# The last layer norm of a two-block transformer kernel: GpSimd takes part of the subtractions, scalings and affine steps, and the stores go out in another order

## What is computed

```python
def layernorm(x, g, b):
    xf = x.astype(jnp.float32)
    mu = jnp.mean(xf, axis=-1, keepdims=True)
    var = jnp.mean(jnp.square(xf - mu), axis=-1, keepdims=True)
    y = (xf - mu) * lax.rsqrt(var + LN_EPS)
    return (y * g + b).astype(x.dtype)
...
    hid = jnp.square(jax.nn.relu(jnp.einsum('bsd,df->bsf', x, w_ff1)))
    ff = jnp.einsum('bsf,fd->bsd', hid, w_ff2)
    return layernorm(DEEPNORM_ALPHA * x + ff, ln2_g, ln2_b)
```

## Time and profile before

| | us |
|---|---|
| median of 3 runs (2074.2 to 2076.59) | 2075.11 |
| the profiled execution | 2075.19 |
| its span | 2073.4 |
| TensorE busy | 2037.0 |
| VectorE busy | 1233.0 |
| ScalarE busy | 977.0 |
| GpSimd busy | 299.3 |

### The profile page before, as it was taken

One profiled execution on the slowest core, in us unless ns is written; L12 is line 12 of the kernel. 1 busy time (PEld: TensorE's weight loads), 2 busy tenths in 40 slices (PEclk: granted clock), 3 DMA queues, 4 the chain that ended last, 5 costly groups with the idle time before them and its releaser, 6 DMA issues. The chain is left out here.

```text
span 2073.4 us, 26672 instructions
## 1 busy us (share of the span) xinstructions
PE 2037.0 (98%) x10608; PEld 1719.8 (83%) x10608; DVE 1233.0 (59%) x1978; ACT 977.0 (47%) x1606; POOL 299.3 (14%) x279
## 2 busy tenths in 40 slices
PE   9999999999999999999999999999999999999997
PEld 6888788888888888788788799898788788899896
DVE  6655566555443444476576475577676586466576
ACT  5664344334232332366357263464566357264363
POOL 0000000000000000254000234130354000233220
PEclk9999999999999999999999999999999999999999
DMA  7332223333332322633332241332532331242331
GB/s 242 98 106 63 82 62 101 122 102 121 103 102 95 98 92 62 179 107 96 100 102 80 82 140 62 104 122 63 167 110 84 117 102 62 82 142 62 122 102 41
DMA packets 201528, 211.51 MB, mean 102 GB/s; under 512 B 7803, under 2 KB 181115, under 8 KB 201404
## 3 DMA queue, kind: packets, MB, share of 16 engines
q1 hardware_dynamic: 194544, 194.13, 29.9%
q0 software_dynamic: 6352, 15.24, 2.8%
q10 hardware_dynamic: 508, 0.43, 0.1%
HBM read 194.55 MB, written 8.95 MB: 98 GB/s over the span
## 5 line engine op out<-in xcount | busy, mean ns | idle before, releaser
L678 PE MATMUL ps<-Phi,wh 128*128 128x512 f32 (+1 forms) x992 | 393.3, 396 | 5.0 <-DVE x_fvv L1343 2.0
L681 PE MATMUL ps<-Phi,wl 128*128 128x512 f32 (+1 forms) x992 | 372.6, 376 | 0.6 <-DVE wl L1257 0.6
L679 PE MATMUL ps<-Plo,wh 128*128 128x512 f32 (+1 forms) x992 | 371.8, 375 | 0.0
L1257 DVE TENSOR_TENSOR wl<-stage,wh 128x1024 fp32r<-128x1024 f32 (+1 forms) x246 | 305.6, 1249 | 65.4 <-ACT wh L2089 46.7
L2089 ACT ACTIVATE wh<-stage 128x1024 fp32r<-128x1024 f32 (+3 forms) x249 | 251.0, 1020 | 98.0 <-PE ps L681 76.1
L678 PE MATMUL ps<-Qhi,wh 128*128 128x512 f32 (+1 forms) x664 | 254.5, 383 | 9.0 <-DVE Qlo L1276 9.0
L679 PE MATMUL ps<-Qlo,wh 128*128 128x512 f32 (+1 forms) x664 | 253.0, 381 | 0.0
L681 PE MATMUL ps<-Qhi,wl 128*128 128x512 f32 (+1 forms) x664 | 252.7, 381 | 0.0
L678 PEld LDWEIGHTS ps<-Phi,wh 128*128 128x128 f32 x992 | 187.3, 189 | 46.6 <-issue 12.4
L681 PEld LDWEIGHTS ps<-Phi,wl 128*128 128x128 f32 x992 | 186.7, 188 | 35.8 <-DVE wl L1257 1.0
L679 PEld LDWEIGHTS ps<-Plo,wh 128*128 128x128 f32 x992 | 187.3, 189 | 31.7 <-issue 4.1
(11 more groups left out here) (351 smaller groups left out, 4077.6 us busy)
## 6 DMA issues: line engine op xcount, KB each, us to landing
stage<-in_w_ff SPq DMA_DIRECT2D x64, 1024.0 KB, 5.4
stage<-in_w_in SPq DMA_DIRECT2D x39, 1024.0 KB, 5.3
stage<-in_w_up SPq DMA_DIRECT2D x16, 1024.0 KB, 5.4
stage<-in_w_down SPq DMA_DIRECT2D x16, 1024.0 KB, 5.1
stage<-in_w_in SPq DMA_DIRECT2D x30, 512.0 KB, 4.9
stage<-in_w_out SPq DMA_DIRECT2D x12, 1024.0 KB, 5.0
stage<-in_w_bg SPq DMA_DIRECT2D x4, 1024.0 KB, 5.2
vrev<-H SPq DMA_DIRECT2D x2, 2048.0 KB, 13.9
```

Source lines behind the costliest of these rows:

```text
L678: e.matmul(o, hi[:, k, cs_], hi_x[:, kx, tok], start=k == 0, stop=False)
L679: e.matmul(o, hi[:, k, cs_], lo_x[:, kx, tok], start=False, stop=False)
L681: t = e.matmul(o, lo[:, k, cs_], hi_x[:, kx, tok], start=False, stop=k == nk - 1)
L1257: t = e.tensor_tensor(lo, src, hi.bitcast(F32), ALU.subtract)
```

## The change

It touches N = 3 only.

- GpSimd does `minus` and then `times` for tiles 4 to 7 of the first half, `minus` for tiles 6 and 7 of the second half, and at the end the affine step of these two tiles.
- VectorE keeps the rest. Its second-half `times` go through the tiles in the order 6, 0, 1, 7, 2, 3, 4, 5, the two on tiles 6 and 7 waiting for GpSimd, and it does the affine step of tile 5, second half.
- ScalarE does the affine step of tiles 0 to 7 of the first half and 0 to 4 of the second; that of tile 4, first half, stands ahead of `part(2, 1)`, that is of tile 7's square, and tile 5's ahead of `scale(1)`.
- SyncE stores the second half's pairs in the order (0, 1), (6, 7), (2, 3), (4, 5) and waits at the end for the last of them.

```diff
@@ vector: times
-                        on.wait_ge(act_norm["scale", N, hf], vec_norm["minus", N, k, hf])
+                        apart = N == 3 and k > 5
+                        on.wait_ge(act_norm["scale", N, hf], (pool if apart else vec_norm)["minus", N, k, hf])
@@ vector: last_three
                 if not nxt:
-                    minus(0, 4, 5)
                     times(0, 0, 1, 2, 3)
                     part(1, 1)
                     add_squares(N)
                     part(2, 1, False)
-                    minus(0, 6, 7)
                     mean(1)
-                    times(0, 4)
                     squared.clear()
+                    minus(1, 0, 1)
                     variance(1)
-                    times(0, 5)
-                    minus(1, 0, 1)
-                    times(0, 6)
-                    minus(1, 2, 3)
-                    times(0, 7)
-                    minus(1, 4, 5, 6, 7)
-                    times(1, *range(8))
+                    minus(1, 2, 3, 4, 5)
+                    times(1, 6, 0, 1, 7, 2, 3, 4, 5)
+                    on.wait_ge(vec_norm["times", N, 5, 1])
+                    t = e.tensor_scalar(H[:, 5, HALVES[1]], d8[:, 5, HALVES[1]], prm[:, V_LN2G + 13:V_LN2G + 14],
+                                        prm[:, V_LN2B + 13:V_LN2B + 14], ALU.mult, ALU.add)
+                    t.then_inc(*vec_norm.up("final", N, 5, 1))
                     return
@@ scalar: last_three
                     times(0, 0, 1, 2, 3)
                     part(1, 1)
+                    times(0, 4)
                     part(2, 1)
                     mean(1)
-                    times(0, 4)
+                    times(0, 5)
                     scale(1)
-                    times(0, 5, 6, 7)
-                    times(1, *range(8))
+                    times(0, 6, 7)
+                    times(1, 0, 1, 2, 3, 4)
@@ gpsimd, at its end
+            def minus(hf, *ks):
+                sl = HALVES[hf]
+                for k in ks:
+                    on.wait_ge(act_norm["mean", 3, hf], vec_norm["deviation", 3, k, None if k < 5 else hf],
+                               act_norm["square", 3, k, None if k < 5 else hf])
+                    t = e.tensor_tensor(d8[:, k, sl], H[:, k, sl], muB[:, sl], ALU.subtract)
+                    t.then_inc(*pool.up("minus", 3, k, hf))
+
+            minus(0, 4, 5, 6, 7)
+            for k in (4, 5, 6, 7):
+                on.wait_ge(act_norm["scale", 3, 0], pool["minus", 3, k, 0])
+                t = e.tensor_tensor(d8[:, k, HALVES[0]], d8[:, k, HALVES[0]], rB[:, HALVES[0]], ALU.mult)
+                t.then_inc(*pool.up("times", 3, k, 0))
+            minus(1, 6, 7)
+            for k in (6, 7):
+                on.wait_ge(vec_norm["times", 3, k, 1])
+                t = e.tensor_scalar(H[:, k, HALVES[1]], d8[:, k, HALVES[1]], prm[:, V_LN2G + 8 + k:V_LN2G + 9 + k],
+                                    prm[:, V_LN2B + 8 + k:V_LN2B + 9 + k], ALU.mult, ALU.add)
+                t.then_inc(*pool.up("final", 3, k, 1))
@@ sync
-            for k0, n, hf in ((0, 4, 0), (4, 4, 0), (0, 2, 1), (2, 2, 1), (4, 2, 1), (6, 2, 1)):
+            last = {(5, 1): vec_norm, (6, 1): pool, (7, 1): pool}
+            for k0, n, hf in ((0, 4, 0), (4, 4, 0), (0, 2, 1), (6, 2, 1), (2, 2, 1), (4, 2, 1)):
...
-            on.wait_ge(stored[6, 1])
+            on.wait_ge(stored[4, 1])
```

More of the change, by code:

```diff
@@ L2487, in times @@
                         c = 8 * (N // 2) + k
-                        on.wait_ge(vec_norm["times", N, k, hf])
+                        on.wait_ge((pool if N == 3 and hf == 0 and k > 3 else vec_norm)["times", N, k, hf])
                         t = e.activation(H[:, k, sl], d8[:, k, sl], ACT.Identity, bias=prm[:, b + c:b + c + 1],
@@ L2809, in sync @@
                         e.dma_start(H[:, :, :], parking).then_inc(*back_in.up("in", L, by=16))
-            for k0, n, hf in ((0, 4, 0), (4, 4, 0), (0, 2, 1), (2, 2, 1), (4, 2, 1), (6, 2, 1)):
+            last = {(5, 1): vec_norm, (6, 1): pool, (7, 1): pool}
+            for k0, n, hf in ((0, 4, 0), (4, 4, 0), (0, 2, 1), (6, 2, 1), (2, 2, 1), (4, 2, 1)):
                 sl = HALVES[hf]
-                on.wait_ge(*(act_norm["final", 3, k, hf] for k in range(k0, k0 + n)))
+                on.wait_ge(*(last.get((k, hf), act_norm)["final", 3, k, hf] for k in range(k0, k0 + n)))
                 e.dma_start(ov[:, k0:k0 + n, sl], H[:, k0:k0 + n, sl]).then_inc(*stored.up(k0, hf, by=16))
-            on.wait_ge(stored[6, 1])
+            on.wait_ge(stored[4, 1])
         Signal.counting = True
```

## The result

The changed kernel takes 2081.46 us (median of 9 runs, 2079.78 to 2083.19) where the kernel before, run beside it, takes 2075.11 (median of 9 runs, 2073.76 to 2076.59): 1.0031 times the time, 95% interval 1.0020 to 1.0041. It is slower by 0.31%. The forecast was 2078.1 in a range of 2073.5 to 2080.2, so the time lies above the range. The profiled execution took 2079.78 us for a span of 2078.0; it is the lowest of the nine.

A forecast was written before the change was run, and what follows sets the result against it. It took VectorE's queue, then ScalarE's rate, to bound the tail behind TensorE's last product. 3.95 - 1.21 - 0.58 + 0.82 = +2.98 us on 2075.1 gave 2078.1 us, range 2073.5 to 2080.2.

The forecast's parts named there:

- step 3: From the last H to the second half's qB: 1.63 us before and after, so no change.
- 0.4 us more is the span's end: After the last store lands: the span ends 0.4 us later, with no difference forecast for the change.
- 1. woven first-half `minus`: First half, under the products: four GpSimd `minus` alternate with VectorE's four, making rB 2.2 us later.
- 2. woven `times`: First-half `times`: three handovers to GpSimd cost +1.65 us and a held-up accq 0.1 before the last H.
- 4. qB to the last group of `times`: Second half, qB to its first `times`: 3.82 us instead of 5.03, two handovers included, so -1.21.
- Steps 5 and 6: The end: last store issued after 3.93 us instead of 4.5 (-0.58), then crowded stores land later (+0.82).
- The rhythm: GpSimd gets its turn after each VectorE two-input operation: 0.89 us between VectorE starts instead of 0.34; chance 0.50.
- VectorE keeps its turn: Rival: GpSimd comes on only where VectorE idles or reads PSUM; last H at 2060.17, time 2076.6 us; chance 0.28.
- no collision: Rival: GpSimd and VectorE don't hinder each other in this tail, H and qB stay; time 2073.0 us; chance 0.14.
- the dear weave: Rival: every handover costs more than 0.55 us, from about 0.86 us per GpSimd tile; 2080.7 at 1.0; chance 0.08.
- step 5: First second-half `times` to the last store's issue: VectorE's `times`, with two GpSimd affine steps between, 3.93 us, -0.58.
- the first case: Main case: VectorE and GpSimd alternate at about 0.74 us per GpSimd tile; own range 2077.3 to 2079.2; chance 0.50.

The follow-up runs named there:

- after_warm: The changed kernel with five more matrix products, results unread, in TensorE's idle time before its second-half sums; 2080.83 us, ratio 1.0027.
- second_half: The kernel before with only the change's second-half part: GpSimd subtracts and affines tiles 6 and 7; 2077.89 us, ratio 1.0012.
- after_again: The changed kernel run once more, unchanged, for a second trace; 2082.08 us, ratio 1.0032 to the kernel before.
- affine_back: The changed kernel with GpSimd's two affine steps (tiles 6 and 7, second half) given to VectorE; 2078.58 us, ratio 1.0018 to the kernel before.
- spare_scales: The kernel before plus eight one-input GpSimd operations (scale and offset, 128x256) into spare memory that nobody waits for; 2078.67 us, one run.

## Why the prediction was wrong, step by step

The forecast of +2.98 us was made against the profiled execution of before. The chain is the one that was forecast, and five of its six steps are right within 0.2 us. Two steps failed: step 3 ("Nothing") was off by half a microsecond, and the end, "0.4 us more is the span's end", by more than two.

| step | forecast | measured |
|---|---|---|
| 1. woven first-half `minus`, until the `times` start | +2.2 | +2.17 (6.42 instead of 4.25) |
| 2. woven `times`, until the last H | +1.75 | +1.66 |
| 3. last H to qB | 0 | +0.49 |
| 4. qB to the last group of `times` | -1.21 | -1.26 (3.75 instead of 5.01) |
| 5. and 6. from there until the last store has landed | +0.24 | +0.08 |
| from the last landing to the span's end | 0 | +2.15 |
| sum | +2.98 | +5.29 |

*The rhythm (steps 1, 2, 4) was right.* GpSimd's four `minus` take 3.61 us, 0.90 each, against the forecast pitch of 0.89, so 0.74 us for a GpSimd tile fits, though no trace has an undisturbed one, and GpSimd does get its turn after each of VectorE's operations. The rivals "VectorE keeps its turn" (last H at 2060.17, that is 8.2) and "no collision" (7.6) both fall by 11.46; so does the dear weave, which would need more than 0.86 us per tile.

*Step 3 failed on the clock.* "1.63 us before and after" took TensorE's sum at 0.70 us. I had followed VectorE's lateness to the second, and wrote that TensorE "has been done for five microseconds by then", and didn't ask what this idle time does to TensorE. By the windows and by after_warm the lower clock costs 0.49 us.

*Steps 5 and 6 were right, step 5 in part by luck.* The last store is issued 3.93 us after the last group of `times` begins (2068.62 to 2072.55), as forecast, before 4.52. But ScalarE and VectorE are through at 2072.19 and 2072.23, 3.6 us after it where 3.89 was worked out, and SyncE comes to the last issue 0.3 us after them: the pair (6, 7), which waits for GpSimd until 2071.51, and (2, 3) are issued at 2071.54 and 2071.95 ahead of it. The last issue, by SyncE's timeline, and the median us from issue to landing of the four small stores:

```profile
2072.55 0.45 SPq L2834 DMA_DIRECT2D out_T<-H  x1
```
```profile
out_T<-H SPq DMA_DIRECT2D x2, 512.0 KB, 3.0
out_T<-H SPq DMA_DIRECT2D x4, 256.0 KB, 2.7
```

It lands after 2.9 us, where 2.2 + 0.82 = 3.0 was worked out. GpSimd's two affine steps delay VectorE's eight `times` by 0.4 us in all (3.16 against 2.77), 0.2 each instead of 0.33. The steps themselves take 2.37 us for two, where second_half's two, nearly alone, take 1.20: GpSimd is held up as well, and with it its drain.

*The missing term is the largest.* "That gives 2072.97, and 0.4 us more is the span's end" was carried over to the changed kernel as if it were a constant. It holds as long as SyncE is the last to arrive at the barrier. With the change GpSimd is: its last operation ends at 2071.51, its drain 6.2 us later, and the last store has landed at 2075.4. The row was in the trace of before, in a place where it cost nothing and where no view of waits points to it. Without it the stretch would be about 24.55 against 21.42, so +3.13 where +2.98 was forecast. That this is so close is partly luck: step 3's +0.49 is nearly made up by 0.34 us that the other steps together came out lower.

*The rest.* The stretch explains 5.29 us of the 6.35 between the medians. So the 3.36 us by which 2081.46 lies above 2078.1 are 2.15 for the drain, 0.49 for the clock, 0.34 less for the other steps, and 1.06 that lie outside the stretch, where the prediction had no difference. The profiled execution of after reached its first qB 0.69 us sooner than that of before and took 4.59 us longer. In all fourteen traces the first qB starts between 2050.6 and 2053.7 us with the same instructions ahead of it. One place at which they differ is a piece in which the clock is granted at the lower level for a time. Windows of before, of after and of after_again:

```profile
1760.00:1775.00 15.00, 11.15 (x42) 9.09 (x43) 10.78 (x11) 5.09 (x6) 1.58 (x1) 0.89 0.46 143
```
```profile
1760.00:1775.00 15.00, 11.61 (x45) 9.52 (x46) 10.31 (x11) 4.64 (x6) 2.18 (x1) 0.89 0.49 152
```
```profile
1760.00:1775.00 15.00, 10.66 (x37) 8.30 (x36) 11.40 (x12) 6.16 (x8) 0.50 (x1) 0.77 0.44 141
```

With 0.77 the same work gets less far in the 15 us (37 matmuls instead of 42 and 45). It is not the only such place: by GpSimd's rows, which come in the same order in every trace, after_again is 0.1 us behind before at 973 us, 1.3 behind at 1181, 1.1 at 1575 and 1.75 at 1812, the same 1.75 as at the first qB. Between 1100 and 1180 us its granted clock is lower too (1150 to 1180: 0.97 against 1.00).

The 1.06 us aren't told apart from noise in one comparison, but they don't look like chance of a session. The difference of the medians less that of the stretches is 1.06 for the changed kernel, 1.72 for after_again and 0.88 for after_warm, and between -0.4 and +0.7 for the nine other kernels that were timed more than once, second_half in the session of the last two and affine_back, which differs from the changed kernel in two operations, among them. The mean granted clock goes with it in part: 0.996 in the profiled execution of after, 0.992 or 0.993 in its other eight, and 0.995 or 0.996 for the kernel before beside the experiments. So the profiled execution is the odd one of the nine. Why the changed kernel, whose difference lies far behind these places, should fall on the long form more often is not explained, and these 1.1 us stay open.

The chances were wrong for the same reason as the sum. "only the dear weave and some of the first case's upper end lie above 2079.3" listed only ways in which the terms of the sum could be mis-sized, and none in which one was missing. "Slower", beyond 2079.3, had 0.09 and came; "same" had 0.90.

## What to carry to other kernels

Before work is given to an engine that has been idle at the end, look up when its own closing instructions end in the trace: here GpSimd's drain ended 6.2 us after its last operation, so that an operation within some 6 us of the last landing set the end of the program. GpSimd and VectorE operations that both have two SBUF inputs take turns: by the four `minus`, a 128x256 tile moved from VectorE (0.34 us) to GpSimd cost VectorE 0.54 us instead. In this norm such a move could pay only where VectorE idles, reads PSUM or waits for something else; second_half, with its drain taken off, is the one case, by an estimated 0.4 us. When a chain gets later, ask of each engine that now idles for it what its first work will then cost.

## What the runs showed that was not expected

- GpSimd's closing drain ends 6.2 us after its last operation, within 0.1, in all fourteen traces, whether that is a 128x512 add, a 128x256 affine step or a 128x64 write.
- Which of GpSimd's operations hinder VectorE: per four, adds make 1.42 us into 3.59, one-input scales into 2.23, memsets leave 1.43.
- A 128x256 TENSOR_SCALAR with constants takes GpSimd 0.56 us beside VectorE's work, while the row gives 0.92 for x_bi's and the changed kernel's two took 2.37, second_half's 1.20.
- VectorE's affine step of 128x256 takes 0.41 us, as much as an operation with two inputs, not less.
- TensorE's clock behind a short rest: after 3.57 us without work, 0.70 of work and 0.87 without, the granted clock of the stretch was 0.51, and the two matmuls of the sum took 1.20 us; with 2.32 us of matmuls in that rest they took 0.70. In spare_scales a rest of 1.15 us was followed by 1.22 too.
